# Hybrid encoder step: gates between the logarithms, second convolution first, and the second feed-forward stage's norm sums behind product 4

## What is computed

```python
x = x + 0.5 * swiglu(rms_norm(x, n_f1), wg1, wu1, wd1)
h = rms_norm(x, n_mix) @ w_in
u_a, v_a, b_b, c_b, x_b, q_c, k_c, v_c, r_c, g_low = jnp.split(h, SPLIT_IDX, axis=-1)
y_a, v_rows = gmlp_mix(u_a, v_a, w_s, b_s)
y_b, conv_new = short_conv(b_b, c_b, x_b, conv_hist, conv_w)      # b * conv3(c * x_in)
y_c, s_new = gla_mixer(q_c, k_c, v_c, r_c, g_low, ...)            # rms_norm per head, times silu(r)
x = x + jnp.concatenate([y_a, y_b, y_c], axis=-1) @ w_o
x = x + 0.5 * swiglu(rms_norm(x, n_f2), wg2, wu2, wd2)
gate = jax.nn.sigmoid(rms_norm(x, n_ple) @ w_ple_gate)
x = x + gate * (p @ w_ple_proj)
```

## Time and profile before

| | |
|---|---|
| median of 3 runs | 1982.15 us (1981.54 to 1984.12) |
| the profiled execution | 1977.9 us, of which the span is 1976.0 us |
| PE busy in the span | 1928.6 us (98%) |
| DVE, ACT, POOL busy | 1295.5, 744.5, 111.7 us |
| mean granted TensorE clock | 0.995 of full speed |

### The profile page before, as it was taken

One profiled execution on the slowest core, in us unless ns is written; L12 is line 12 of the kernel. 1 busy time (PEld: TensorE's weight loads), 2 busy tenths in 40 slices (PEclk: granted clock), 3 DMA queues, 4 the chain that ended last, 5 costly groups with the idle time before them and its releaser, 6 DMA issues.

```text
span 1976.0 us, 36256 instructions
## 1 busy us (share of the span) xinstructions
PE 1928.6 (98%) x14738; PEld 1905.1 (96%) x14738; DVE 1295.5 (66%) x1807; ACT 744.5 (38%) x1064; POOL 111.7 (6%) x79
## 2 busy tenths in 40 slices
PE   8899999999999999999999989999999999999998
PEld 8899999999999999999989989999999999999997
DVE  6966767667776874244436587666676786868624
ACT  7533333335242454111153363333333352433514
POOL 1200000000000002011040110000000000000121
PEclk9999999999999999999999999999999999999999
DMA  5232232326451532111022032333223255441302
GB/s 196 82 102 81 90 131 81 102 81 230 152 197 39 164 114 74 44 43 29 26 92 90 29 108 82 119 102 102 81 81 130 92 197 200 144 164 39 97 22 88
DMA packets 142829, 203.36 MB, mean 103 GB/s; under 512 B 5760, under 2 KB 116048, under 8 KB 139280
## 3 DMA queue, kind: packets, MB, share of 16 engines
q1 hardware_dynamic: 142736, 202.03, 30.4%
HBM read 147.10 MB, written 54.91 MB: 102 GB/s over the span
## 4 chain that ended last, share of the span: by engine, by line
PE 85%; DVE 8%; ACT 3%; DMA 2%; issue 2%; SPq 0%; DVEq 0%; ACTq 0%
PE ps L2588 60%; PE ps L2526 21%; DMA op_raw<-h_ops 2%; DVE wr_lo L1663 1%; PE ps L2642 1%; DVE op_lo L1803 1%; DVE x L1912 1%; DVE xl L2347 1%; PE ps L2551 0%; PE ps L2859 0%; PE ps L2879 0%; DMA xin_a<-in_x_prompt 0%; PE ps L2754 0%; PE ps L2885 0%; PE ps L2816 0%
## 5 line engine op out<-in xcount | busy, mean ns | idle before, releaser
L2588 PE MATMUL ps<-op_hi,wr_hi 128*128 128x264 f32 x3640 | 743.8, 286 | 22.7 <-DVE x L1912 10.5
L2588 PE MATMUL ps<-op_hi,wr_lo 128*128 128x264 f32 x3640 | 744.0, 286 | 0.0
L2588 PE MATMUL ps<-op_lo,wr_hi 128*128 128x264 f32 x3640 | 742.5, 285 | 0.0
L2588 PEld LDWEIGHTS ps<-op_hi,wr_hi 128*128 128x128 f32 x3640 | 567.8, 189 | 28.8 <-DVE x L1912 13.3
L2588 PEld LDWEIGHTS ps<-op_hi,wr_lo 128*128 128x128 f32 x3640 | 566.0, 189 | 0.0
L2588 PEld LDWEIGHTS ps<-op_lo,wr_hi 128*128 128x128 f32 x3640 | 564.6, 189 | 0.0
L1091 ACT ACTIVATE wr_hi<-wr_raw 128x512 fp32r<-128x512 f32 (+1 forms) x268 | 164.6, 619 | 380.7 <-DVE wr_raw L1673 159.7
L2526 PE MATMUL ps<-xh,wh 128*128 128x352 f32 x912 | 206.4, 331 | 6.1 <-DVE xl L2347 3.4
L2526 PE MATMUL ps<-xh,wl 128*128 128x352 f32 x912 | 198.5, 323 | 0.0
L1663 DVE TENSOR_TENSOR wr_lo<-wr_raw,wr_hi 128x512 fp32r<-128x512 f32 (+1 forms) x268 | 176.5, 682 | 30.0 <-ACT wr_hi L1091 18.4
L1091 ACT ACTIVATE wr_hi<-wpair 128x512 fp32r<-128x512 f32 (+1 forms) x201 | 123.2, 615 | 147.1 <-PE ps L2588 141.2
(11 more groups left out here) (276 smaller groups left out, 1653.0 us busy)
## 6 DMA issues: line engine op xcount, KB each, us to landing
h_ops<-hq SPq DMA_DIRECT2D x22, 1848.0 KB, 7.0
op_raw<-h_ops SPq DMA_DIRECT2D x28, 1056.0 KB, 8.7
wpair<-in_w_ffn_up SPq DMA_DIRECT2D x22, 1024.0 KB, 5.3
wpair<-in_w_ffn_gate SPq DMA_DIRECT2D x21, 1024.0 KB, 9.0
wpair<-in_w_ffn_down SPq DMA_DIRECT2D x16, 1024.0 KB, 7.7
wst<-in_w_in SPq DMA_DIRECT2D x22, 512.0 KB, 3.8
op_raw<-h_ops SPq DMA_DIRECT2D x14, 792.0 KB, 5.1
wpair<-in_w_ffn_down SPq DMA_DIRECT2D x8, 768.0 KB, 4.5
```

The source lines that it names most:

```text
L2588: last = pe.matmul(ps[:, out + h, 0:TQ], w_[idx][:, m, :], x_[:, n, h * TQ:h * TQ + TQ], start=idx in (0, 1, 3) and m == 0 and w_ is wr_hi ...
```

## The change

Same instructions, in another order (three more table loads follow from it). At the end of the mixers, ACT takes `gate_silu(0)` and `conv_first(1)` before the second head's logarithm, `gate_silu(1)` before the fourth head's, and all seven result tiles in one run behind `gate_silu(2)`, with `gate_silu(3)` ahead of the W_o split; DVE takes `conv(1)` before the o norms, `scale_r(1)` and `scale_r(2)` each before the next o norm, and `scale_r(3)` after five result tiles. In the feed-forward stage, PE makes product 4 before `norm_means(2)`, and ACT takes `norm_log(2)` behind `t4_hi(1)` and two rounded weights, directly before `norm_scale(2)`; a wait for the last square takes its old place.

```diff
@@ def first_gate_end(f) of ACT
                 w_op_hi(u + 1, 0)
                 w_op_hi(u + 1, 1)
                 if f > 0:
+                    norm_log(2)
                     norm_scale(2)
@@ ACT, end of the mixers
             split_hi(u_r[2])
             o_log(1)
             o_square(2)
+            gate_silu(0)
+            conv_first(1)
             o_log(2)
             o_square(3)
             for n in range(3):
                 o_scale(n)
-            gate_silu(0)
-            conv_first(1)
             split_hi(u_r[3])
             o_log(3)
             o_square(4)
+            gate_silu(1)
             o_log(4)
             o_scale(3)
             o_scale(4)
-            gate_silu(1)
             split_hi(u_wo[0])
-            y_part(0)
             gate_silu(2)
-            for k in range(1, KT - 1):
+            for k in range(KT - 1):
                 y_part(k)
+            gate_silu(3)
             split_hi(u_wo[1])
-            gate_silu(3)
             y_part(KT - 1)
@@ ACT, first unit of the second feed-forward stage
             first_sum(UNITS, 3, sr[:, 2, :])
-            norm_log(2)
+            act.wait_ge(sq_added, (KT - 1) * 2)
             w_op_hi(UNITS, 6)
             t4_hi(1)
             first_gate_end(1)
@@ DVE, end of the mixers
             scale_r(0)
             conv(0)
             split_lo(u_r[2])
+            conv(1)
             o_norm_samples()
             o_norm(0)
-            conv(1)
             o_norm(1)
             split_lo(u_r[3])
             scale_r(1)
+            o_norm(2)
+            scale_r(2)
+            o_norm(3)
             split_lo(u_wo[0])
-            y_part(0)
-            o_norm(2)
-            o_norm(3)
-            scale_r(2)
-            for k in range(1, KT - 1):
+            for k in range(5):
                 y_part(k)
             scale_r(3)
+            for k in range(5, KT - 1):
+                y_part(k)
             split_lo(u_wo[1])
@@ def up_unit of PE
                 product(u, 3, i, first)
+                pe.wait_ge(act_rd, nth(3, v, 2, i))
+                product(u, 4, i, first)
                 if first:
                     pe.wait_ge(dve_rd, drained(u, 1))
                     norm_means(2)
-                pe.wait_ge(act_rd, nth(3, v, 2, i))
-                product(u, 4, i, first)
```

## The result

| | runs | median us | lowest to highest |
|---|---|---|---|
| kernel before | 5 | 1982.15 | 1981.54 to 1984.12 |
| changed kernel | 5 | 1970.87 | 1969.97 to 1973.66 |

The ratio is 0.995, 95% interval 0.9936 to 0.9964: faster by 11.3 us. The sign was forecast; 6.9 us were, and the range's lower end was 1972.8. The profiled execution of the changed kernel took 1973.66 us (span 1971.4), the one of before 1977.9: between these two only 4.2 us.

The account below looks back on a forecast made before the run. PE, busy 1928.6 of 1976.0 us, was taken as the bound, so only its pauses could be won. The mixers' end gave -6.9 us and the second feed-forward stage 0: 1982.15 to 1975.2 us, range 1972.8 to 1979.1.

Parts of the forecast that it names:

- The mixers' end: End of the mixers to step 7 of W_o's first tile: step 7 starts at 1052.8 instead of 1059.69, -6.9 us.
- Gate 2's silu: ACT at the mixers' end: runs from 1034.5 instead of 1043.00, since `scale_r(2)` is ready by 1033.7.
- tile 7's lo part: DVE at the mixers' end: the lo part that PE's step 7 needs ends at 1052.7.
- the bound where PE alone decides: Mixers' end: if ACT and DVE are 1 us quicker, only PE sets the end, -7.1 us.
- the fourth logarithm: ACT at the mixers' end: stays at 1027.77, when PE's sums come; gate 1 and its load just fit ahead.
- Pauses and slow clock: PE at the mixers' end: pauses of 1.88, 1.96 and 1.41 us plus 1.7 us lost to the clock, together 6.95 us.
- The second stage: Second feed-forward stage: sum 0; bounds are a gain of 1.06 us and losses of 1.0 and 1.7 us.
- Rival 1: Second feed-forward stage costs: clock falls at product 6's wait, up to 1.7 us, or POOL's exclusion, 1.0; 1976.2 to 1976.9; chance 0.14.
- a fall behind the new pause: Second feed-forward stage: the clock may fall at the 2.6 us wait before product 6, up to 1.7 us.
- The three table loads: ACT at the mixers' end: nine loads instead of six, 3.85 us of ACT alone, already counted in the steps.
- The step that failed: Whole kernel: the median's 4.25 us above the profiled execution taken as it is, 1982.15 - 6.9 = 1975.2 us.

Follow-up runs that it names:

- conv_dve: Kernel before with gate 0's silu, the second convolution's first tap and conv(1) put ahead, plus VectorE's new order; ScalarE's gate 1 stays behind the logarithms: one execution, 1978.37 us.

## Why the prediction was right or wrong

**The mixers' end: right in mechanism, 0.6 us too small.** Gate 2's silu, the tiles and tile 7's lo part came within 0.6 us of the forecast. The term is 7.53 us instead of 6.9, and beyond the -7.1 that I gave as the bound where PE alone decides. Of the 0.6, 0.4 came with PE: the fourth logarithm, which waits for PE's norm sums, runs at 1027.4 where I kept 1027.77 as given. The sums themselves had been held by ACT's last square. Before, it ended at 1025.70, and PE's sums began at 1025.75:

```profile
1024.65 1.05 ACT L1425 ACTIVATE osq<-mix 128x1024 f32<-128x1024 f32 x1
```

In the changed kernel it ends 2.45 us ahead of the sums:

```profile
1023.89 1.05 ACT L1426 ACTIVATE osq<-mix 128x1024 f32<-128x1024 f32 x1
```

```profile
1027.39 1.88 PE L2552 MATMUL ps<-osq,ones 128*128 128x512 f32 x4
```

**Pauses and slow clock added up, for a reason that I had only half.** I wrote 5.25 us of pauses and 1.7 of slow clock. Filling the old pauses removed the slow clock and brought nothing that could be measured; the two are one bound, the end of ACT's and DVE's chain. Only a fall behind the last pause adds to it, 1.6 us in one trace.

**The second stage: 0, as forecast,** term by term, when it is held against the one trace that I had. Rival 1 came in part, with 0.6 to 0.8 us in two traces of three where the clock fell behind the longer pause. What I left out is the other side: I priced a fall behind the new pause and none behind the old one for `hq`, and in three of six traces the old order has one there, which costs it 1.5 us.

**The three table loads** are there (4.0 us of ACT, 1.28 each) and are hidden. Here the rule of the Trainium skill (ScalarE: Activation LUTs, "Table sets: the hidden batching unit") that functions of one set go together would have cost most of the gain: conv_dve keeps gate 1 behind the logarithms and has one more load than before instead of three, and its step 7 is 4.6 us later (ACT's other two moves are missing in it too).

**The step that failed** is the last one, from the profiled execution to the median: "The median of the runs shown is 1982.15, 4.25 us above that execution; I take the difference as it is", with a range whose lower end allowed the "1.3 us by which the runs shown differ around their median". The difference of the two kernels, 6.9 us, was nearly right, but three runs told neither the median nor the spread. Over all that ran here, 81 executions of the kernel before have a median of 1981.4 (1976.96 to 1985.88), and 20 of the changed one 1973.4 (1968.69 to 1979.05). That is 8.0 us: 7.5 at the mixers' end, and a rest that is within what 20 executions can tell. The five first ones were 2.5 us low for the changed kernel and 0.7 high for the other, and 8.0 + 2.5 + 0.7 are the 11.3 us. The first result's own interval, 7.1 to 12.7 us, holds 8.0. So the change is worth about 7 to 8 us (7.2 without the first five), and 1970.87 was not the middle of the changed kernel. That the first five were low by chance is the reading that is left, and it is not shown: five executions drawn from the 15 later ones have a median of 1970.87 or less in about 2 of 100 draws, and medians of five drawn from all 81 and from all 20 are 11.3 us or more apart in 6 of 100. The later runs were on two chips; the record does not name the chip of the first result, so a difference between chips is not ruled out.

What the executions differ by is shown in part. Each fall of the clock behind a pause of about 2 us that nothing later takes up costs 1.5 to 1.6 us (behind step 7 and behind the pause for `hq`; I had reckoned with 1.7), and which pauses have one changes from trace to trace (four falls in the first trace of before, seven in the second). And the up projections run at two rates. PE's row over the same 400 us of the second stage, in the first and the second trace of before:

```profile
1190.00:1590.00 400.00, 400.00 (x3290) 400.00 (x3289) 278.22 (x432) 142.31 (x236) 0.91 (x1) 1.00 0.30 102
```

```profile
1190.00:1590.00 400.00, 400.00 (x3271) 400.00 (x3270) 277.87 (x430) 140.91 (x233) 3.64 (x3) 1.00 0.29 97
```

19 matmuls fewer at the same clock and with no pause are 2.3 us. They are not missing records, since both traces hold all 14738: the same 600 matmuls in a row take 73.00 us in the first trace and 73.42 in the second. Of the 14 traces, 5 have the higher rate there, of either kernel. What sets it stays open; so does the spread that is left with filled pauses (8 us at mean clocks of 0.997 to 0.999).

**The best version** that ran is the changed kernel with its pauses filled: 1968.6 and 1967.9 us, 5 us below the changed kernel and 13 below the one before.

## What to carry to other kernels

When a chain on two helper engines sets the end, a new place for one instruction pays only if both engines' orders let it through: here the convolution alone brought a tenth of the gain, and VectorE's queue stood 10.37 us at a split that waited for the other engine. Measure a local change between two events that both traces have; that gave 7.5 us to a few hundredths, and showed the one trace that differs, where five whole runs gave 11.3 and nine gave 6.5. Take more than one trace of the old kernel too: a fall of the clock that one trace has and another lacks was worth 1.5 us at either place. And ahead of a range, ask how far single executions of the same kernel lie apart; three of them do not say.

## What was not expected of the hardware

- Matmuls of ones in a pause kept the granted clock at 1.00 behind every pause that had them, in all five traces. Both kernels were about 5 us faster with fills outside the mixers' end; the three fills at the mixers' end won nothing.
- A pause of the same length is followed by a fall in one execution and not in another: 2.14 us at 54 us had one in the first trace of the changed kernel and none in the second; 1.71 to 1.75 us for `hq` had one in three traces of six.
- The same loop ran 3290 or 3271 matmuls in 400 us at a granted clock of 1.00, by the execution and not by the kernel.
